# AdaLN gate vectors of a two-layer trunk: split accumulator and fp32r products with ones in place of fp32 products

## What is computed

```python
c_act = jax.nn.silu(c)
for i in range(DEPTH):
    mod = c_act @ ada_w[i] + ada_b[i]
    sh_mix, sc_mix, g_mix, sh_mlp, sc_mlp, g_mlp = jnp.split(mod, N_MOD, axis=-1)
    h = modulate(rmsnorm(x, norm_mix[i]), sh_mix, sc_mix)
    mix = fox_mixer(...) if i == 0 else short_conv_mixer(...)
    x = x + g_mix[:, None, :] * mix
    h = modulate(rmsnorm(x, norm_mlp[i]), sh_mlp, sc_mlp)
    x = x + g_mlp[:, None, :] * sq_relu_mlp(h, mlp_w_up[i], mlp_w_down[i])
return rmsnorm(x, final_norm)
```

## Time and profile before

| | us |
|---|---|
| median of 3 runs | 2337.84 |
| lowest, highest | 2334.38, 2339.28 |
| span of the profiled execution | 2332.3 |
| PE busy | 2275.7 (98%) |
| DVE busy | 1649.4 (71%) |
| ACT busy | 1054.5 (45%) |
| gate sums on PE (L504), 8 of them | 1.72 each in the chain |

### The profile page before, as it was taken

How to read it: one execution, slowest core, us unless ns; L and a number is a source line. 1 busy time by engine, 2 the same in 40 slices (tenths; PEclk the granted TensorE clock), 3 DMA queues, 4 the chain that set the end, 5 groups by cost and what they waited for, 6 DMA issues and landing times.

```text
span 2332.3 us, 28846 instructions
## 1 busy us (share of the span) xinstructions
PE 2275.7 (98%) x11203; PEld 1919.9 (82%) x11203; DVE 1649.4 (71%) x1562; ACT 1054.5 (45%) x1190; POOL 172.7 (7%) x339
## 2 busy tenths in 40 slices
PE   5999999999999999999999999999999999999998
PEld 5999998878888888888877888887888888888886
DVE  6888999867857857857867887766785455455455
ACT  4444344454444434434445444445443543443443
POOL 0001121101101101101100111100110000000000
PEclk8999999999999999999999999999999999999999
DMA  9987999959959968968967888855986555556563
GB/s 363 386 316 254 336 349 346 369 174 319 333 192 313 328 205 290 327 223 276 326 219 247 312 311 312 315 186 168 316 303 196 183 188 193 190 188 194 184 203 122
DMA packets 270529, 615.60 MB, mean 264 GB/s; under 512 B 14704, under 2 KB 15040, under 8 KB 269504
## 3 DMA queue, kind: packets, MB, share of 16 engines
q1 hardware_dynamic: 220480, 437.56, 54.8%
q0 software_dynamic: 46080, 167.79, 20.1%
q10 hardware_dynamic: 3840, 8.42, 1.0%
HBM read 611.62 MB, written 2.10 MB: 263 GB/s over the span
## 4 chain that ended last, share of the span: by engine, by line
PE 91%; DVE 3%; DMA 2%; issue 2%; ACT 1%; SPq 0%; DVEq 0%; ACTq 0%
PE ps L465 27%; PE ps L467 27%; PE ps L466 26%; PE ps L452 2%; PE ps L453 2%; PE ps L454 2%; DMA start_ring<-in_ada_w_dram 2%; PE ps L766 1%; DVE acc L1294 1%; PE ps L507 1%; PE ps L504 1%; DVE w_lo L1279 0%; DVE square_out L1294 0%; PE ps L541 0%; ACT w_hi L837 0%
## 5 line engine op out<-in xcount | busy, mean ns | idle before, releaser
L1279 DVE TENSOR_TENSOR w_lo<-raw,w_hi 128x1024 fp32r<-128x1024 f32 x724 | 883.9, 1224 | 556.9 <-ACT w_hi L837 555.1
L837 ACT ACTIVATE w_hi<-raw 128x1024 fp32r<-128x1024 f32 x724 | 766.6, 1060 | 1083.2 <-PE ps L467 1028.0
L465 PE MATMUL ps<-w_hi,h 128*128 128x512 f32 x1536 | 607.6, 396 | 5.5 <-DVE h L1396 4.0
L467 PE MATMUL ps<-w_lo,h 128*128 128x512 f32 x1536 | 601.2, 391 | 0.0
L466 PE MATMUL ps<-w_hi,h 128*128 128x512 f32 x1536 | 600.7, 391 | 0.0
L465 PE MATMUL ps<-w_hi,mid 128*128 128x512 f32 x1280 | 502.9, 393 | 0.0
L467 PE MATMUL ps<-w_lo,mid 128*128 128x512 f32 x1280 | 498.9, 390 | 0.0
L466 PE MATMUL ps<-w_hi,mid 128*128 128x512 f32 x1280 | 498.6, 390 | 0.0
L465 PEld LDWEIGHTS ps<-w_hi,h 128*128 128x128 f32 x1536 | 290.1, 189 | 67.4 <-issue 8.3
L467 PEld LDWEIGHTS ps<-w_lo,h 128*128 128x128 f32 x1536 | 289.7, 189 | 61.0
L466 PEld LDWEIGHTS ps<-w_hi,h 128*128 128x128 f32 x1536 | 290.3, 189 | 58.6 <-issue 0.5
(11 more groups left out here) (216 smaller groups left out, 1258.5 us busy)
## 6 DMA issues: line engine op xcount, KB each, us to landing
ada_raw<-in_ada_w_dram POOLq DMA_DIRECT2D x320, 512.0 KB, 6.3
raw<-in_mlp_w_up_dram SPq DMA_DIRECT2D x128, 1024.0 KB, 5.3
raw<-in_mlp_w_down_dram SPq DMA_DIRECT2D x128, 1024.0 KB, 6.4
raw<-in_fox_w_in_dram SPq DMA_DIRECT2D x48, 1024.0 KB, 10.5
raw<-in_conv_w_in_dram SPq DMA_DIRECT2D x48, 1024.0 KB, 7.5
start_ring<-in_ada_w_dram SPq DMA_DIRECT2D x64, 512.0 KB, 12.2
raw<-in_fox_w_out_dram SPq DMA_DIRECT2D x16, 1024.0 KB, 10.2
raw<-in_conv_w_out_dram SPq DMA_DIRECT2D x16, 1024.0 KB, 5.2
```

The lines of the kernel that those rows point to most:

```text
L465: mm(o, xh, hi, start=(k == first), stop=False)
L467: last = mm(o, xh, lo, start=False, stop=(k == end - 1))
L837: op(w_hi[:, e % WR], raw[:, e // 2, EK * (e % 2):EK * (e % 2 + 1)], ACT.Copy).then_inc(hi_ready, 1)
L1279: v.tensor_tensor(w_lo[:, e % WR], raw[:, e // 2, EK * (e % 2):EK * (e % 2 + 1)], w_hi[:, e % WR].bitcast(F32), ALU.subtract).then_inc(spl ...
```

## The change

- ACT copies the float32 ones into an fp32r matrix `ones_r` once, before the output projection.
- Two slots ahead of each gate sum, ACT rounds the accumulator to fp32r: `gate_parts[:, 0]` (`round_gate`), after its split of slot s - 2.
- One slot ahead, DVE writes the remainder `gate_parts[:, 1] = accumulator - gate_parts[:, 0]` (`low_gate`), after its split of slot s - 1 and before that slot's steps.
- PE waits for the remainder and then makes four fp32r products of 128x512 with `ones_r` where it made two float32 products.
- `gate_parts` takes the memory of the attention's `ks`, so the first rounding waits for the attention's last product (`pv_done`). The slots of the sums, the plans and all DMAs stay as they were.

```diff
                 pe.wait_ge(ada_steps, KC * (i + 1))
                 pe.wait_ge(mod_ready, i)
                 if is_gate:
+                    pe.wait_ge(ones_ready, 1)
+                    pe.wait_ge(gate_low, gates_before(i) + 1)
                     for b in range(2):
-                        last = mm(ps[:, SUM - 1 + b, :], ones[:, :], accs[slot][:, NU * b:NU * (b + 1)], start=True, stop=True)
+                        mm(ps[:, SUM - 1 + b, :], ones_r[:, :], gate_parts[:, 0, NU * b:NU * (b + 1)], start=True, stop=False)
+                        last = mm(ps[:, SUM - 1 + b, :], ones_r[:, :], gate_parts[:, 1, NU * b:NU * (b + 1)], start=False, stop=True)
...
+            def round_gate(i):
+                if i == A_GATE0:
+                    act.wait_ge(pv_done, NG)
+                act.wait_ge(ada_steps, KC * (i + 1))
+                act.wait_ge(ada_summed, i)
+                op(gate_parts[:, 0, :], accs[i % 2], ACT.Copy).then_inc(gate_hi, 1)
...
+            op(ones_r[:, :], ones[:, :], ACT.Copy).then_inc(ones_ready, 1)
...
+            def low_gate(i):
+                dve.wait_ge(gate_hi, gates_before(i) + 1)
+                v.tensor_tensor(gate_parts[:, 1, :], accs[i % 2], gate_parts[:, 0, :].bitcast(F32), ALU.subtract).then_inc(gate_low, 1)
...
+        def ahead(table, first, slots):
+
+            return {s - slots: first + i for s, i in table.items() if is_gate(first + i)}
...
-                body(at(U_CONV + i), None, stores(CONV_STORE, i, conv_store, extra), PLAN_CONV[0][i], A_CONV)
+                hooks = joined(ahead(CONV_SUM, A_CONV, 1), i, low_gate, stores(CONV_STORE, i, conv_store, extra))
+                body(at(U_CONV + i), None, hooks, PLAN_CONV[0][i], A_CONV)
```

More of the change, by code:

```diff
@@ L129, in build @@
             ("upto", [P, TT, T], F32), ("wf", [P, KC, H], F32), ("wf_hi", [P, KC, H], F32R), ("wf_lo", [P, KC, H], F32R)])
-        _, conv_b, conv_c, _, gate = over([
+        _, conv_b, conv_c, gate_parts, gate = over([
             ("at_qs", [P, 2, QK, NU], F32), ("conv_b", [P, NB, T], F32), ("conv_c", [P, TT, NU], F32),
-            ("to_vs", [P, QK, NU], F32), ("gate", [P, D], F32)])
+            ("gate_parts", [P, 2, NA], F32R), ("gate", [P, D], F32)])
         ada_raw = sb("ada_raw", [P, TILES, NA])
@@ L174, in build @@
         causal = sb("causal", [P, P], F32R)
+        ones_r = sb("ones_r", [P, P], F32R)
         ones = sb("ones", [P, P])
@@ L230, in build @@
         ada_steps = sem("ada_steps")
+        gate_hi = sem("gate_hi")
+        gate_low = sem("gate_low")
+        ones_ready = sem("ones_ready")
         ada_summed = sem("ada_summed")
@@ L352, in build, with is_gate, gates_before, joined @@
         CONV_SUM, CONV_STORE = sums_of(PLAN_CONV)
+        def is_gate(i):
+            return isinstance(i, int) and PARTS[ADA[i][0]] in GATE
+        def gates_before(i):
+            return sum(is_gate(j) for j in range(i))
+        def ahead(table, first, slots):
+            return {s - slots: first + i for s, i in table.items() if is_gate(first + i)}
+        def joined(table, n, call, hooks=None):
+            hooks = dict(hooks or {})
+            for e in range(NE):
+                if NE * n + e in table:
+                    i = table[NE * n + e]
+                    other = hooks.get(e)
+                    hooks[e] = (lambda i=i, other=other: [other and other(), call(i)])
+            return hooks
         @block.sync
@@ L1164, in load_root @@
                 op(square_out[:, 0:1], recip[:, 0:1], ACT.Sqrt)
+            op(ones_r[:, :], ones[:, :], ACT.Copy).then_inc(ones_ready, 1)
             for n in range(NG):
                 residual(at(U_OUT0 + n), n, R_OUT0, 1,
-                         ({3: first_gate}, {3: load_root}, None, None)[n],
+                         joined(ahead(QKV_SUM, 0, 2), U_OUT0 + n, round_gate, ({3: first_gate}, {3: load_root}, None, None)[n]),
                          first=None if n else {0: lambda: round_probs(NG - 1)})
@@ L1186, in round_hidden, with mlp_slice @@
                    ACT.Copy).then_inc(hid_hi, 1)
-            def mlp_slice(base, s, l, norm_before=None, gate_part=None, norm_after=None, last=False):
+            def mlp_slice(base, s, l, norm_before=None, gate_part=None, norm_after=None, last=False, gate_first=None):
                 hid = SLICES * NG * l + NG * s
@@ L1198, in mlp_slice @@
                         hooks[3] = lambda: round_hidden(n - 1, hid + n - 1)
+                    if gate_first is not None:
+                        hooks = joined(ahead(SLICE_SUM, gate_first, 2), n, round_gate, hooks)
                     body(un, None, hooks)
@@ L1205, in mlp_slice @@
                         final[0] = load_final
+                    if gate_first is not None:
+                        final = joined(ahead(SLICE_SUM, gate_first, 2), NG + n, round_gate, final)
                     residual(at_mlp(base, s, NG + n), n, r0, norm_after, final, last=last and n == NG - 1)
@@ L1210, in load_final @@
                               ).then_inc(final_arrived, 16)
-            mlp_slice(U_MLP0, 0, 0, norm_before=1, gate_part=5)
+            mlp_slice(U_MLP0, 0, 0, norm_before=1, gate_part=5, gate_first=A_MLP0)
             with act.Fori(1, SLICES - 1) as s:
@@ L1260, in _ @@
                     hooks[7] = lambda: conv_copy(i)
-                body(at(U_CONV + i), None, hooks)
+                body(at(U_CONV + i), None, joined(ahead(CONV_SUM, A_CONV, 2), i, round_gate, hooks))
             for n in range(NG):
@@ L1264, in _ @@
                          None if n else {1: lambda: conv_last_tap(NG - 1), 2: lambda: conv_round(NG - 1)})
-            mlp_slice(U_MLP1, 0, 1, norm_before=3, gate_part=5)
+            mlp_slice(U_MLP1, 0, 1, norm_before=3, gate_part=5, gate_first=A_MLP1)
             with act.Fori(1, SLICES - 1) as s:
@@ L1797, in _ @@
                 first = None if n else {0: lambda: low_probs(NG - 1)}
-                residual(at(u), n, R_OUT0, 1, stores(QKV_STORE, u, qkv_store, extra), PLAN_QKV[0][u], 0, first=first)
+                hooks = joined(ahead(QKV_SUM, 0, 1), u, low_gate, stores(QKV_STORE, u, qkv_store, extra))
+                residual(at(u), n, R_OUT0, 1, hooks, PLAN_QKV[0][u], 0, first=first)
             def low_hidden(n, hid):
@@ L1819, in mlp_slice @@
                     hooks = extra if store is None else stores(SLICE_STORE, n, store, extra)
+                    if isinstance(i0, int) and is_gate(i0):
+                        hooks = joined(ahead(SLICE_SUM, i0, 1), n, low_gate, hooks)
                     steps = None if store is None else PLAN_SLICE[0][n]
```

## The result

| | before | changed |
|---|---|---|
| median of the runs, us | 2336.70 (4 runs, 2334.38 to 2339.28) | 2346.84 (4 runs, 2346.19 to 2349.32) |
| ratio, with its 95% interval | | 1.0048 [1.0036, 1.0059] |
| span of the profiled execution, us | 2332.3 | 2344.5 |

The changed kernel is slower by 0.48%: 11.2 us by the ratio, 12.2 by the spans. The forecast was 7.7 us over the kernel before, 2345.6 us, with a range of 2339.2 to 2350.4, which holds 2346.84.

The account below looks back on a forecast made before the run. PE, busy 98% of the span, was taken to bound the kernel. Waits of 14.2 us against 6.5 gained make 7.7 us slower: span 2340.0, plus 5.5 to the median, 2345.6 us; range 2339.2 to 2350.4.

Parts of the forecast that it names:

- The gain on PE: At each of 8 gate sums, four fp32r products replace two float32 ones: 0.81 us less each, 6.5 us in all.
- The waits: PE waits for DVE's remainder ahead of the gate sums: 14.2 us in all, from 0.2 at sum 6 to 4.2 at sum 5.
- Sum 2: At gate sum 2, PE comes 2.35 us late, DVE runs without a break 1.2 late; wait 2.3 us.
- The release: From the end of a DVE operation to the start of the product it releases on PE: 0.15 us.
- The clock: Rival: PE's clock falls to half in the longest wait, sum 5's, costing 2.4 us; time 2348.0 us; chance 0.28.
- This lateness alone costs nothing: After a sum, DVE's 1.13 us delay per subtraction stays inside the three slots for which PE's weights are split ahead.
- No later wait of PE gives it back: At the norms PE waits for DVE's work on its own last pair, which moves with it, so the loss stays.
- Lateness smaller: Rival: DVE no later at sums 1, 2 and 5 than at 3 and 4; waits 7.9 us, time 2339.2 us; chance 0.12.
- No wait at all: Rival: rounding and remainder ready when PE arrives at the gate sums, only the 6.5 us gain left; 2331.4 us; chance 0.08.
- No gain from fp32r: Rival: a gate sum's four products take as long as the two they replace, waits remain; 2352.0 us; chance 0.06.

Follow-up runs that it names:

- e6: Changed kernel with gate sums again by two float32 products, keeping PE's wait and ACT's and DVE's new work; ratio 1.0078, 18.2 us slower than the kernel before.
- e1: Changed kernel with 12 and 17 unread dummy products on PE ahead of its waits at gate sums 1 and 5; ratio 1.0038, median 2346.10 us.
- e4: e3 with sum 1's remainder one slot further ahead, sum 2 moved to (14, 2), sum 5 to (4, 4); ratio 0.9987, 3.0 us faster than the kernel before.
- e3: Changed kernel with rounding and remainder each one slot earlier, three and two slots ahead of each gate sum; ratio 1.0001 to the kernel before.
- e2: Changed kernel with gate sum 5 alone made by two float32 products without the wait, ACT's and DVE's work kept; ratio 1.0024, 5.6 us over the kernel before.
- e5: Changed kernel with gate sums again by two float32 products and no wait, ACT's and DVE's new work still made; ratio 1.0006, median 2337.79 us.
- e7: Changed kernel without the wait, its fp32r products reading a constant part of h, so gate rows are not the accumulator's sums; ratio 0.9994.
- e9: e4 with sum 2 back at (13, 7), its rounding at (13, 1), remainder at (13, 2), item 5's sum at (15, 1); ratio 0.9973, median 2328.87 us.
- e10: e9 with the two float32 products of the accumulator in place of the four fp32r products; ratio 0.9999, median 2335.20 us.
- e8: e5 with item 5's sum moved three slots later, from (14, 6) to (15, 1); ratio 0.9995, median 2334.43 us.

## Why the prediction was right

- **The gain on PE**, 0.81 us a sum and 6.5 in all: right. Sums that don't wait gain 0.86, since the unit's products right behind an fp32 sum start 0.23 to 0.24 apart for over a microsecond and return to 0.227 only then; behind fp32r products they don't need to. Behind a sum that waited it is the same as behind an fp32 one, so that there 0.81 is the better number.
- **The waits**, 14.2 us: right, term by term; on sum 2 see the next point. Sum 1 3.16, measured 3.17; sum 2 2.34, 2.41; sums 3, 4, 7 and 8 1.08 or 1.09, 1.08; sum 5 4.21, 4.21; sum 6 0.2, 0.16. The steps that carried this, ACT's and DVE's start after PE's pair, and DVE's backlog at sums 1 and 5, stand. e6 shows their whole price with nothing to set against them, 18.2 us with the clock's falls.
- **Sum 2** agrees partly by luck. The forecast had PE 2.35 us late there and DVE 1.2. In the changed kernel both were 1.7 later than that, PE 4.0 and DVE 2.9, since the fall after sum 1, which the forecast's sum leaves out, slowed the pair that DVE's next split waits for; the wait between them stayed. In e1, without the fall, that split came when the forecast had it, at 412.8 by the start times of before, but a tile was late on the way and the wait was 3.07. That DVE runs without a break from there is the step that doesn't always hold: the prediction has the tiles come later and counts no wait for them.
- **The release**, 0.15 us: right, 0.15 at sum 1. What the sum didn't hold is the 0.07 by which the second product of a sum that waited is late: 0.6 us in all.
- **The clock**, the first rival, held at 0.28: it came true as well, twice. The forecast's sum left it out. It was sized at 2.4 us a fall, from twelve products at the half level, and 1.6 were lost, since nine products fall into the half-rate stretch. The two falls, 3.2 us, are most of the 3.5 us by which the ratio's 11.2 exceeds the forecast's 7.7. That the median 2346.84 lies only 1.2 us above the forecast's 2345.6 is luck: the kernel before had 2336.70 beside it, 1.1 under the 2337.84 that the forecast started from. The cost was under-sized by a third, by a term that the prediction had named and put outside its sum.
- The Trainium skill ("TensorE: Matmul & The Clock Gate", section "Why this matters for your kernels") has about 3 us as the idle gap to stay below between bursts of matmuls. By that rule sum 1 (3.17) and sum 5 (4.21) are exposed and sum 2 (2.41) not, and the changed kernel's trace agrees in all three. Other runs don't: the clock fell after e4's 2.72 us, and it stayed full after 3.07 in e1 and 3.44 in e3. There the measurements decide: the rule is a warning and not a boundary.
- **"This lateness alone costs nothing"** was wrong, though it cost nothing here. It held at the gate sums (e2, e5: shift 0.00), and at item 5's sum in the changed kernel, where the shift even fell by 0.23 us. But the waits hid it: PE came late itself. Without them, e5 lost 2.9 us there and e7 5.6. I had looked at the split's three slots of reserve and not at the steps that a sum of another item waits for.
- **"No later wait of PE gives it back"**: right within what can be told, -0.3 us over the norms and item 5's sum.
- **The other rivals.** Lateness smaller: no, sums 1, 2 and 5 waited as read. No wait at all: e9 is that case, made by hand, 6.3 us faster than before by its ratio; the changed kernel isn't. No gain from fp32r: no, e9 against e10.

## What to carry to other kernels

A product made cheaper by splitting its operand on other engines is worth only as much as those engines have lead at its slot: read, for each place, when the producer could end there against when PE arrives, since the mean load of DVE (71%) said nothing and a wait of 1.1 us at the best places already took the whole gain of 0.86. Moving the producer one slot ahead doesn't cure every place: in e3, at sum 5, the rounding's new place held up ACT's own split. When a wait is removed, look which lateness it had been hiding: here that was another item's sum, which took 5.6 of the 6.9 us gained in e7 and more than the net gain of e3. Where a wait of some microseconds can't be avoided on a PE that is otherwise always busy, dense products in it kept the clock up in e1, though its times don't confirm the saving; better is to move the consumer and the producer, which gave 0.27% over the kernel before.

## What the runs showed of the hardware that I had not expected

- The clock mostly fell not in the wait but after it, when PE was already back at full work: 0.8 to 1.0 us later in the changed kernel, in e4 0.4 us later. In e2 and e6 it was down already when PE resumed at sum 1, in e6 for 0.9 us. In e2 PE's timeline has half the usual pace from the first product on:

```profile
407.81 0.77 PE L535 MATMUL ps<-gate_parts,ones_r 128*128 128x512 f32 x1 [3.01 <-DVE gate_parts L1357]
408.37 0.63 PE L536 MATMUL ps<-gate_parts,ones_r 128*128 128x512 f32 x1
408.80 0.63 PE L535 MATMUL ps<-gate_parts,ones_r 128*128 128x512 f32 x1
```

- The length of the wait alone does not say whether it falls. It fell after 2.72 us (e4), stayed full after 2.41 (sum 2 of the changed kernel), after 3.07 (sum 2 of e1, where the profile has a wait of 2.91 and the windows from 439.5 to 444 all show 1.00), and even after 3.44 (sum 5 of e3). After 3.17 at sum 1 it fell in all three runs that have this wait with PE idle, and after 4.21 at sum 5 in both. What tells these apart was not settled; one profiled execution of each can't say whether the same kernel does the same each time.
- The clock also fell after short waits with sparse work behind them: in e5 after 1.5 us of wait (1.31 by the profile) and then sixteen one-column products of 1.8 us, in e3 after 0.9 us of wait and the same products, at gaps that don't look dangerous by themselves. In the trace of before, with 0.15 us of wait ahead of them, it stayed full. A fall ahead of dense work cost 1.6 us each time at the gate sums of the changed kernel and 2.9 at sum 1 of e6; at item 5's sum in e7, where it lasted from 456.0 to 462.8, wait and fall together cost 5.6.
- The start of the kernel passes up to 2.5 us differently in executions of code that is the same there: against before, 0.0 us in e5, 0.94 in the changed kernel, 2.06 in e8 and 2.5 in e6. Spans should be compared from the end of the execution, or from a place after the start.
